# The first experts of the four columns get a table of their own, written ahead of the table of all blocks

## The reference, cut to what matters

```python
def hierarchical_moe(h, wg, bg, we, be, w_gate, w_up, w_down):
    g_star = jnp.argmax(p_group, axis=-1)
    ...
    top_v, top_i = lax.top_k(p_exp, TOP_K)            # TOP_K = 2
    expert_idx = g_star[:, None] * EXPERTS_PER_GROUP + top_i
    combine = jnp.sum(jax.nn.one_hot(expert_idx, 16) * weights[..., None], axis=1)
    a = jnp.einsum("nd,edf->nef", hf, w_gate)         # 1024 -> 256
    b = jnp.einsum("nd,edf->nef", hf, w_up)
    u = jax.nn.silu(a) * b * combine[..., None]
    return jnp.einsum("nef,efd->nd", u, w_down)       # 256 -> 1024
```

## Time and profile before

| | us |
|---|---|
| median of 3 runs | 1906.14 |
| lowest, highest | 1904.08, 1909.82 |
| profiled execution | 1904.11 |
| its span in the trace | 1902.3 |
| PE busy in the span | 1739.9 (91%) |
| DVE busy | 557.7 (29%) |

### The profile page before, as it was taken

How to read it: one execution, slowest core, us unless ns; L and a number is a source line. 1 busy time by engine, 2 the same in 40 slices (tenths; PEclk the granted TensorE clock), 3 DMA queues, 4 the chain that set the end, 5 groups by cost and what they waited for, 6 DMA issues and landing times. The chain is left out here.

```text
span 1902.3 us, 19532 instructions
## 1 busy us (share of the span) xinstructions
PE 1739.9 (91%) x7811; PEld 823.9 (43%) x7811; DVE 557.7 (29%) x1092; ACT 389.2 (20%) x703; POOL 24.4 (1%) x34
## 2 busy tenths in 40 slices
PE   6998999999998999999999999998999998777892
PEld 4544545554435534444344334433444434343441
DVE  4605403551116011011110239835310204420113
ACT  5102113531012100101000030146500012300112
POOL 0100000000000000000000000000000000010001
PEclk9998999999999999999999999999999999888996
DMA  9711264111321999999999912211021131199965
GB/s 368 249 44 44 97 235 177 45 67 44 133 83 68 406 422 426 420 422 421 422 427 420 382 53 88 89 44 45 2 88 65 67 133 66 78 316 367 321 217 187
DMA packets 91821, 382.61 MB, mean 201 GB/s; under 512 B 10644, under 2 KB 10980, under 8 KB 76644
## 3 DMA queue, kind: packets, MB, share of 16 engines
q1 hardware_dynamic: 82084, 350.14, 47.5%
q10 hardware_dynamic: 5632, 16.78, 2.8%
q0 software_dynamic: 4032, 14.68, 2.0%
HBM read 466.51 MB, written 18.87 MB: 255 GB/s over the span
## 5 line engine op out<-in xcount | busy, mean ns | idle before, releaser
L1758 PE MATMUL bank<-H,weight_slots 128*128 128x512 f32 (+1 forms) x1024 | 426.4, 576 | 4.7 <-ACT H L685 2.9
L1758 PEld LDWEIGHTS bank<-H,weight_slots 128*128 128x128 f32 x1024 | 197.4, 194 | 226.6 <-issue 220.2
L1758 PE MATMUL bank<-R,weight_slots 128*128 128x512 f32 x576 | 252.5, 597 | 4.4 <-DVE R L1296 2.1
L1758 PEld LDWEIGHTS bank<-R,weight_slots 128*128 128x128 f32 x576 | 109.1, 191 | 144.3 <-issue 134.8
L2084 PE MATMUL bank<-weight_slots,SM 128*64 128x512 f32 x640 | 143.9, 595 | 9.4 <-DMA weight_slots<-in_w_up_e 9.4
L2419 PE MATMUL bank<-weight_slots,SM 128*32 128x256 f32 x1536 | 99.1, 416 | 35.1 <-DMA weight_slots<-in_expert_w_gate 21.9
L2112 PE MATMUL bank<-weight_slots,SM 128*64 128x512 f32 x384 | 114.7, 610 | 3.6 <-DMA weight_slots<-in_w_down_e 3.6
L1758 PE MATMUL bank<-R 128*128 128x128 f32 (+2 forms) x784 | 104.9, 288 | 9.7 <-DVE R L1655 6.2
L1758 PEld LDWEIGHTS bank<-R 128*128 128x128 f32 x784 | 96.0, 198 | 13.2 <-issue 10.7
L2084 PEld LDWEIGHTS bank<-weight_slots,SM 128*64 128x64 f32 x640 | 45.4, 137 | 104.2 <-issue 84.2
L2419 PEld LDWEIGHTS bank<-weight_slots,SM 128*32 128x32 f32 x1536 | 54.8, 120 | 79.0 <-issue 41.3
(11 more groups left out here) (422 smaller groups left out, 1522.3 us busy)
## 6 DMA issues: line engine op xcount, KB each, us to landing
weight_slots<-in_expert_w_gate SPq DMA_DIRECT2D x51, 1024.0 KB
weight_slots<-in_expert_w_up SPq DMA_DIRECT2D x51, 1024.0 KB
R<-in_expert_w_down SPq DMA_DIRECT2D x51, 1024.0 KB
weight_slots<-in_w_up_e SPq DMA_DIRECT2D x24, 2048.0 KB, 17.3
weight_slots<-in_w_down_e SPq DMA_DIRECT2D x24, 2048.0 KB, 23.6
weight_slots<-in_w_in SPq DMA_DIRECT2D x18, 2048.0 KB, 10.1
weight_slots<-in_w_gate_e SPq DMA_DIRECT2D x16, 2048.0 KB, 17.0
weight_slots<-in_w_ada SPq DMA_DIRECT2D x12, 2048.0 KB, 10.7
```

The source lines that it names most:

```text
L1758: ins = nc.tensor.matmul(dst, lhsT, rhs, start=(i == 0), stop=(i == len(pairs) - 1))
```

## The change

VectorE works out, right behind `first_block`, two rows of four numbers: `first_expert`, the expert of the first block of each column, and `first_change`, whether it differs from the guess. They need five instructions, which stand ahead of `token_slot` and all that follows. SP waits for them (`first_tables`) instead of `block_tables` before it reads the registers of the corrections, and waits for `block_tables` after it has issued these. The table of all 48 blocks is worked out as before. Six signals that had semaphores of their own (`hu_ready`, `ln_sq`, `xa_in`, `gains1`, `gains2`, `gain_both`) and `first_hits` now count in the shared ones of their engine; the waits on them name the same events.

```diff
+        first_expert = ctx.enter_context(nc.sbuf_tensor("first_expert", [1, NSLOT], I32))
+        first_change = ctx.enter_context(nc.sbuf_tensor("first_change", [1, NSLOT], I32))
...
-            sp.wait_ge(*reached("block_tables", 1))
+            sp.wait_ge(*reached("first_tables", 1))
...
-            here = [block_of_step(0, i) for i in range(NSLOT)]
+            here = [(bass.ds(sp.value_load(first_expert[0:1, i:i + 1], min_val=0, max_val=E2 - 1), 1),
+                     sp.value_load(first_change[0:1, i:i + 1], min_val=0, max_val=1)) for i in range(NSLOT)]
             for half in range(2):
                 for i in range(1, NSLOT):
                     load_half(i, half, *here[i])
+            sp.wait_ge(*reached("block_tables", 1))
...
+            tt(first_begun, iota[0:1, 0:4 * NQUAD:NQUAD].unsqueeze(2).broadcast_to([1, NSLOT, E2]), first_block[0:1, :].unsqueeze(1).broadcast_to([1, NSLOT, E2]), ALU.is_gt)
+            step(nc.vector.reduce_sum(first_row, first_begun, AX_X))
+            step(nc.vector.tensor_scalar(first_row, first_row, -1.0, None, ALU.add))
+            step(nc.vector.tensor_copy(first_expert[:, :], first_row))
+            nc.vector.tensor_tensor(first_change[:, :], first_row, first[0:1, :], ALU.not_equal).then_inc(sem("first_tables"), 1)
...
-                pe.wait_ge(sem("first_hits"), 3)
+                pe.wait_ge(*reached("first_hits", 3))
```

More of the change, by code:

```diff
@@ L88 @@
     ("xT_ev", 8), ("k_silu", 8), ("v_ev", 6), ("u_ev", 4), ("gate_s", 3), ("rows_s", 3), ("q_silu", 4), ("o_ev", 4), ("C0_ev", 4), ("Z_ev", 4), ("fu_ev", 4),
-    ("yf_ev", 8), ("ym_ev", 8), ("brb_ev", 8), ("htok_ev", 8), ("km_ev", 4), ("vm_ev", 2), ("glu_ev", 4), ("v2_ev", 4),
-    ("q2_ev", 4), ("k2_ev", 4), ("c_ready", 4), ("ga_ev", 8),
+    ("yf_ev", 8), ("ym_ev", 8), ("brb_ev", 8), ("htok_ev", 8), ("km_ev", 4), ("vm_ev", 2), ("hu_ready", 8), ("glu_ev", 4), ("v2_ev", 4),
+    ("q2_ev", 4), ("k2_ev", 4), ("ln_sq", 4), ("c_ready", 4), ("ga_ev", 8), ("xa_in", 8),
     ("x_sq", 8), ("x_root", 1), ("h_rows", 4),
 ]
-VECTOR_STAGES = [("u_fold", 12), ("kw_ev", 16), ("aff_v", 5), ("router_w", 1), ("glu_s", 2), ("a_s", 2), ("f_v", 5), ("c_v", 1),
-                 ("xtok_v", 8), ("x_ss", 1), ("x_inverse", 1), ("chosen", 1), ("token_slots", 2), ("block_tables", 1), ("out_sum", 8)]
+VECTOR_STAGES = [("gains1", 2), ("u_fold", 12), ("kw_ev", 16), ("gains2", 1), ("aff_v", 5), ("gain_both", 1), ("router_w", 1), ("glu_s", 2), ("a_s", 2), ("f_v", 5), ("c_v", 1),
+                 ("xtok_v", 8), ("x_ss", 1), ("x_inverse", 1), ("chosen", 1), ("first_tables", 1), ("token_slots", 2), ("first_hits", 3), ("block_tables", 1), ("out_sum", 8)]
 def bases(stages):
@@ L374, in build @@
         column_row = const[:, CONST["column_row"]:CONST["column_row"] + NSLOT]
+        first_begun = R7[0:1, 2304:2304 + NSLOT * E2].rearrange("p (c e) -> p c e", c=NSLOT)
+        first_row = R7[0:1, 2304 + NSLOT * E2:2304 + NSLOT * (E2 + 1)]
         pos_in = R7[:, 2256:2256 + 2 * TT * NSLOT].rearrange("p (a t c) -> p a t c", a=2, c=NSLOT)
@@ L835, in _ @@
             pair_copies(NPAIR - 1, False)
-            act.wait_ge(sem("gain_both"), 1)
+            act.wait_ge(*reached("gain_both", 1))
             for k in range(KD):
@@ L1105, in _ @@
                                                op0=ALU.add, op1=ALU.mult).then_inc(sem("gains1"), 1)
-            dve.wait_ge(sem("gains1"), 2)
+            dve.wait_ge(*reached("gains1", 2))
             def scaled(name, src, c, width, i):
@@ L1302, in _ @@
                                            op0=ALU.add, op1=ALU.mult).then_inc(sem("gains2"), 1)
-            dve.wait_ge(sem("gains2"), 1)
+            dve.wait_ge(*reached("gains2", 1))
             rms_scale(dve, "n2", lambda k: xT[:, k, :], lambda k: H[:, k, 0:T], T, std[:, 0:T], rstd2[:, 0:T], lambda k: gains[:, 2, k:k + 1])
@@ L1650, in _ @@
                                         ALU.is_equal).then_inc(sem("first_hits"), 1)
-            dve.wait_ge(sem("first_hits"), 2)
+            dve.wait_ge(*reached("first_hits", 2))
             nc.vector.tensor_tensor(first_rows, first_rows, second_rows, ALU.add).then_inc(sem("first_hits"), 1)
@@ L2164, in _ @@
             for k in range(KD):
-                pe.wait_ge(sem("hu_ready"), k + 1)
+                pe.wait_ge(*reached("hu_ready", k + 1))
                 for j in range(4):
@@ L2209, in _ @@
             for k in range(KH):
-                pe.wait_ge(sem("ln_sq"), k + 1)
+                pe.wait_ge(*reached("ln_sq", k + 1))
                 nc.tensor.matmul(b[:, :], ones, ln_sq[:, k % 2, :], start=(k == 0), stop=(k == KH - 1)).then_inc(sem("lnq_mm"), 1)
@@ L2302, in query @@
                 for k in ks:
-                    pe.wait_ge(sem("xa_in"), k + 1)
+                    pe.wait_ge(*reached("xa_in", k + 1))
                     ins = nc.tensor.matmul(xq_bank[h][:, :], wq[:, k, 128 * h:128 * h + 128], H[:, k, 0:T], start=(k == 0), stop=(k == KD - 1))
```

## The result

The changed kernel takes 1909.89 us (median of 18 runs, 1906.87 to 1916.98), the kernel before 1905.75 (18 runs, 1899.12 to 1909.82). The ratio of the two, as estimated from these runs, is 1.0025, 95% interval 1.0015 to 1.0036: 4.8 us slower (the medians alone differ by 4.1), under the 0.3% that was called a difference, but clear of zero. The forecast was 0.8 us faster.

The account below looks back on a forecast made before the run. Two limits side by side: a chain of waits through the corrections, and nearly always busy DMA engines. Step 1 products start 0.8 us earlier, now released by rows; median 1906.14 - 0.8 = 1905.3 us, range 1900.5 to 1910.

Parts of the forecast that it names:

- Five instructions, 1.05 us: VectorE's chain ahead of the scatter: five added instructions delay everything behind them by 1.05 us, bounds 1.05 to 2.5.
- The earlier signal: SP starts its register reads 5.4 us earlier, is ready at 1667.0 against 1675.25; corrections go out some 8 us earlier.
- Two queues share one for one, the scatter's end is put off by the corrections' own 5 us: DMA queues alternate packets; 2.06 MB of corrections inside the scatter delay its end by 5.0 us, less 0.5.
- Step 0: TensorE: step 0 products start 5.1 us earlier, at 1675.6, and 64 take 3.63 us, not 5.99.
- Rows of step 1 land by the median, 7.2 us: ACT's last row load, issued at about 1684.6, lands at 1691.8; seen landings are 3.7 / 7.2 / 10.4 us.
- a sign of being wrong: Products of step 1 starting before 1691 or after 1697, where 1694 was expected, would show the forecast wrong.
- Then 1.09 + 1.4 us to the products: After the rows land, 1.09 us of transposes and 1.4 us for two copies; step 1 products start at 1694.3.
- What is gained must come out of holes: DMA engines are full from 1702.9, so idle time before it, 2.85 us less 1.05, caps the gain at 1.8.
- the rows come too late: Rival: delayed scatter and earlier step 1 weight loads make step 1 rows land late, up to +2.4 us, 1908.5; chance 0.18.
- head start: Rival: the earlier step 0 start, 5.1 us, and better clock, 2.4 us, go through in full: 1898.6; chance 0.12.
- the corrections did get in: Refers to the rival that the scatter's 8 queued DMAs hold the engines, keeping corrections out until done: 1906.5; chance 0.12.

Follow-up runs that it names:

- e5: Changed kernel, but the up and down loads of step 1 wait until the rows of step 1 have landed; ratio to the kernel before 0.9996.
- e3: Changed kernel, but SP issues the gate loads of step 1 only when the rows of step 1 have landed; ratio to the kernel before 1.0020.
- f1: Changed kernel, but the up corrections wait until the scatter has landed, only gate corrections go out early; ratio to the kernel before 0.9995.
- f3: Kernel before the change, but ACT issues the row loads of steps 2 and 3 behind its SiLU of step 0; ratio to the kernel before 1.0025.
- f4: Changed kernel with the five instructions behind the second token_slot and the up corrections held until the scatter has landed; ratio to the kernel before 1.0014.
- f7: Changed kernel with the five instructions behind the second token_slot, and step 1 ups and downs waiting for its rows; ratio to the kernel before 1.0001.
- f5: Changed kernel, five instructions behind the second token_slot, corrections held until TensorE has picked half the step 0 rows; ratio to the kernel before 1.0010.
- f2: Changed kernel with the five instructions moved behind the second token_slot; ratio to the kernel before 1.0002.

## Why the prediction was wrong, point by point

- **Five instructions, 1.05 us.** Right: 0.93 to 0.95. With five sets the scatter starts 5.2 us later, 1.03 us a set.
- **The earlier signal.** Right: the first read took 0.47 us, the next five 0.27 each, and the last two, once the scatter's packets had come, 0.60 and 0.50; the corrections went out at R + 8.9. Forecast was 1667.0 for R = 1658.47, R + 8.5. (Its 3.75 us up to the first packets should be 3.80, which changes nothing.)
- **Two queues share one for one, the scatter's end is put off by the corrections' own 5 us.** Right: 234 packets to 235; loads of rows forecast at 1683.1, found at 1683.05 (0.8 us later, counted from R). Between 1680 and 1682, 0.23 MB of the gates of step 1 also ran beside the last of the scatter, which the sum didn't have.
- **Step 0.** Right: 64 products in 3.66 us, not 5.99; start at R + 16.6 (forecast R + 17.2).
- **Rows of step 1 land by the median, 7.2 us.** This is the step that failed. The fourth took 9.9 us, and step 1 started at 1698.19, past the 1697 that was named as a sign of being wrong. Counted from R, step 1 started 4.7 us later than forecast: 2.7 of them are this landing, 1.7 the later issue of the fourth load (0.8 from the scatter's end, 0.9 because the four took longer to issue), 0.3 the way from landing to products. I had used the median of all 44 loads, and had noted in the rival that SP would now issue its loads of step 1 earlier, but not worked out which stood ahead of which: gates at R + 20.6, ups at 24.2 against rows at 25.4. With the weights of step 1 ahead, the rows' queue moved 0.50 MB from 1686 to 1692 and SP's 1.31 MB. In e5 and e3, where this order is changed, the fourth load lands in 5.7 and 2.8 us: 4 to 7 us less.
- **Then 1.09 + 1.4 us to the products.** Too short: transposes took 1.98 us after TensorE had waited 13.6 us. Its granted clock was 0.50, the lower of its two levels, from 1686 to 1695; where the eight transposes came right behind products, as in before, they took 1.09. The way from landing to products was 2.8 us.
- **"What is gained must come out of holes".** Right as an upper bound, but it is one-sided. A loss needs no room: the hole ahead of step 2 grew from 2.5 us at 0.47 to 7.0 us at 0.04. I had written that this hole "moves with these"; it grows with these.
- **The rival "the rows come too late"** is what happened, at 0.18. Its mechanism, its place and its point (a landing later than 8.0 us) held; its price was too low. At 9.9 us of landing it asks for 1.9 us, and step 1 was 3.9 us late from R: the other 2.0 are the 1.7 of late issue and the 0.3 of slow transposes. The time, 1909.9, lies at the top end of the range.
- **The other rivals** fell: no head start went through, and the corrections did get in.

How far does the loss at step 1 explain the 4.8 us? Over the fourteen kernels with an interval the start of step 2 goes with the measured time somewhat better than that of step 1 does (correlation 0.80 against 0.70; f1 and f3 are the clearest cases), but not closely: f4 and f7 don't fit. The lag isn't simply passed on either: after is 3.7 us behind before at step 2, but 2.8 us at the last down products. In the traces 1.5 us of the 4.4 between before and after come in these. The last down products:

```profile
1867.29 3.67 PE bank L2433 x32
```

```profile
1869.30 5.22 PE bank L2444 x32
```

The first is of before, with a granted clock of 1.00, the second of after, with a mean of 0.70 (0.50 up to 1872.3, then 0.93 and 1.00). Of the 16 traces 5 have 3.6 us there and 11 have 5.0 to 5.3, f1 and f5 as well as after. It isn't tied to a place of the change that I could find; with one trace for each kernel, whether it belongs to the change is open. So the cause of the late step 1 is shown; how much of the 4.8 us it makes is not. That the order of issue carries the loss rests on e5, whose interval lies below that of after.

## What to carry to other kernels

Before you let a load out earlier, list by time what else is issued on any queue of the same engines, and what each thing's landing gates. On full engines an earlier load takes its time from whatever else is in the same stretch, even where the overlap is short, and here those that paid (the scatter, and then the rows) stood on the chain. When a chain gets shorter, look at what its end will issue sooner: here the ups and downs of step 1, and a wait that held them back until the rows were in brought the time back to that of before, but not below it.

## What the runs showed of the hardware that was not expected

- SP's register reads take 0.27 us at the median. In before the eight during the scatter took 0.43 to 0.87 us and the eight behind it 0.26 to 0.27; the longest read of all traces took 1.18 us, in f2.
- A load of 128 KB of rows of step 1 took 9.9 us in after and 2.8 in e3, where the weights of step 1 had not been issued ahead of it on SP's queue. From 1686 to 1692 in after the two queues moved 186 (SP) and 171 (ACT) packets, 1.31 and 0.50 MB.
- The last 32 down products took 3.6 us (before, granted clock 1.00) or 5.2 us (after, 0.70 on the mean), with the same work there.
- In e5 and f7 single instructions of two engines, SP and TensorE, followed each other at 0.7 us for a few us inside the scatter. No row shows why.
